# Dense units shifted in both attention blocks, tile 1 of a gated projection four units behind, rows summed later

## The reference

```python
def first_block(...):
    mod = silu(c) @ w_ada + b_ada                      # six rows of 1024: shifts, scales, gates
    h = modulate(rms_norm(x, g_mix), sh_m, sc_m)
    qa, ka, va, qb, kb, vb, gate_logits = split(h @ w_in)
    oa = moba_attention(qa, ka, va, rel_bias)          # 8 heads, softmax with a bias
    ob = stick_breaking_attention(qb, kb, vb)          # 8 heads, cumulated log sigmoids
    mixed = (g_a * (oa @ w_br_moba) + g_b * (ob @ w_br_sb)) @ w_out
    x = x + gt_m * mixed
    ... gated convolution feed-forward, final norm
def second_block(...):                                 # layer 0 even, layer 1 odd
    for l in range(2):
        x = x + 0.5 * rmsnorm(swiglu(...))
        m = even_mixer(...) or odd_mixer(...)          # even: differential attention, then attention
        x = x + rmsnorm(m)                             # over the top 64 keys of an indexer
        x = x + 0.5 * rmsnorm(swiglu(...))
```

## Time and profile before

| | before |
|---|---|
| median of 3 runs | 1549.98 us (1548.85 to 1555.81) |
| the profiled execution | 1548.18 us, span of its instructions 1546.4 us |
| TensorE matmul busy | 1462.1 us, 95% |
| VectorE, ScalarE, GpSimd busy | 926.5, 735.7, 57.7 us |
| mean granted clock of TensorE | 0.976 |
| DMA | 274.29 MB, 177 GB/s |

### The profile page before, as it was taken

The page is one execution under the profiler, slowest core; times in us unless marked ns, Lnnn a source line. Parts: engine busy times, 40 slices in busy tenths (PEclk is TensorE's granted clock), DMA queues, the critical chain, the costliest instruction groups (busy, mean ns, idle before and its releaser), DMA issues.

```text
span 1546.4 us, 17969 instructions
## 1 busy us (share of the span) xinstructions
PE 1462.1 (95%) x6791; PEld 1198.4 (77%) x6791; DVE 926.5 (60%) x1128; ACT 735.7 (48%) x990; POOL 57.7 (4%) x104
## 2 busy tenths in 40 slices
PE   5998988899998999999789999999999999999998
PEld 5877867688876888877567888878888778788886
DVE  5675667678866644458955654556454455565443
ACT  1555544555553544355444644445444465554441
POOL 2000000000000000013100000000000100000000
PEclk9998989899999999999879999999999999999999
DMA  8964545277652755535214655546555373356550
GB/s 319 322 223 152 197 176 182 80 244 243 218 190 96 245 190 183 175 99 168 102 55 150 219 189 191 190 150 218 190 191 190 123 211 110 136 168 227 181 174 28
DMA packets 180311, 274.29 MB, mean 177 GB/s; under 512 B 6242, under 2 KB 120674, under 8 KB 180226
## 3 DMA queue, kind: packets, MB, share of 16 engines
q1 hardware_dynamic: 176976, 263.45, 50.9%
q0 software_dynamic: 1824, 6.57, 1.4%
q10 hardware_dynamic: 1425, 3.12, 0.6%
HBM read 272.05 MB, written 1.06 MB: 177 GB/s over the span
## 4 chain that ended last, share of the span: by engine, by line
PE 80%; DVE 10%; issue 4%; ACT 4%; DMA 1%; POOL 0%; DVEq 0%; POOLq 0%; SPq 0%; ACTq 0%
PE psum L2030 24%; PE psum L2032 24%; PE psum L2031 24%; DVE w_lo L1652 2%; PE psum L2225 2%; ACT w_hi L1465 1%; DMA raw<-in_w_ada_dram 1%; PE psum L2101 1%; DVE ada_acc L1693 1%; PE psum L2154 1%; PE psum L2153 1%; PE psum L2169 1%; DVE scr L1992 1%; PE psum L2195 1%; PE psum L2196 0%
## 5 line engine op out<-in xcount | busy, mean ns | idle before, releaser
L1652 DVE TENSOR_TENSOR w_lo<-raw,w_hi 128x2048 fp32r<-128x2048 f32 x157 | 358.3, 2285 | 197.1 <-ACT w_hi L1465 196.7
L2030 PE MATMUL psum<-w_hi,hT_hi 128*128 128x512 f32 x1000 | 400.5, 400 | 10.9 <-DVE w_lo L1652 3.5
L2032 PE MATMUL psum<-w_hi,hT_lo 128*128 128x512 f32 x1000 | 392.4, 392 | 0.0
L2031 PE MATMUL psum<-w_lo,hT_hi 128*128 128x512 f32 x1000 | 391.8, 392 | 0.0
L1465 ACT ACTIVATE w_hi<-raw 128x2048 fp32r<-128x2048 f32 x157 | 299.5, 1909 | 161.6 <-PE psum L2032 95.2
L2030 PEld LDWEIGHTS psum<-w_hi,hT_hi 128*128 128x128 f32 x1000 | 189.8, 190 | 57.9 <-issue 16.9
L2032 PEld LDWEIGHTS psum<-w_hi,hT_lo 128*128 128x128 f32 x1000 | 189.5, 189 | 40.7
L2031 PEld LDWEIGHTS psum<-w_lo,hT_hi 128*128 128x128 f32 x1000 | 189.8, 190 | 36.7
L2030 PE MATMUL psum<-w_hi,hc_hi 128*128 128x512 f32 x256 | 101.8, 398 | 4.8 <-DVE hc_lo L1657 4.0
L1652 DVE TENSOR_TENSOR lo_at<-raw,hi_at 128x2048 fp32r<-128x2048 f32 x35 | 80.2, 2291 | 39.1 <-ACT hi_at L1465 39.1
L1652 DVE TENSOR_TENSOR lo_qk<-raw,hi_qk 128x2048 fp32r<-128x2048 f32 (+1 forms) x35 | 79.2, 2264 | 38.6 <-ACT hi_qk L1465 38.6
(11 more groups left out here) (197 smaller groups left out, 2006.6 us busy)
## 6 DMA issues: line engine op xcount, KB each, us to landing
raw<-in_ffn_wg_dram SPq DMA_DIRECT2D x88, 512.0 KB, 3.7
raw<-in_ffn_wu_dram SPq DMA_DIRECT2D x88, 512.0 KB, 4.7
raw<-in_ffn_wd_dram SPq DMA_DIRECT2D x44, 1024.0 KB, 4.9
raw<-in_w_ada_dram SPq DMA_DIRECT2D x24, 1024.0 KB, 5.5
raw<-in_w_up_dram SPq DMA_DIRECT2D x44, 512.0 KB, 5.1
raw<-in_w_in_dram SPq DMA_DIRECT2D x20, 1024.0 KB, 5.1
raw<-in_even_w_in_dram SPq DMA_DIRECT2D x12, 1024.0 KB, 5.0
raw<-in_odd_w_in_dram SPq DMA_DIRECT2D x12, 1024.0 KB, 5.1
```

The source lines that it names most:

```text
L1652: nc.vector.tensor_tensor(lo_of(s), raw_of(s), hi_of(s).bitcast(F32), ALU.subtract).then_inc(lo_ready, 1)
L2030: nc.tensor.matmul(o, a_hi, b_hi, start=start, stop=False)
L2031: nc.tensor.matmul(o, a_hi, b_lo, start=False, stop=False)
L2032: return nc.tensor.matmul(o, a_lo, b_hi, start=False, stop=stop)
```

## The change

- `WIDE` starts at unit 24, so `w_out`'s units can use the two extra slots and be split ahead.
- `sb_heads`: the second filler of a step runs only from the second pair on, and the lists are reordered (13 lists for 14): unit, two row parts, unit; the last gate unit moves between `sb_keep` and `sb_cum` of the last pair. The transposes of the first attention's output move between the two units of the last gate and from banks 6, 7 to 2, 3.
- `ada_next` sums the previous row after the second part of a row instead of after the first.
- `w_out`: all four units are multiplied for tile 0 first; tile 1 of all four stands in the pieces of `cross`, which now prepares the high half of one unit less before tile 0's chain (`early=1`).
- `out_rest`: the transposes stand between tile 0 and tile 1 of one unit.
- Even block: TensorE waits for the indexer's turn at the first `idx` step, not behind the turn; the two units of the second attention's values (`first_of(5)`, `second_of`) and the turn of its keys move into the last steps of the differential attention.

```diff
-WIDE = ((28, 98), (112, 182), (194, 227))
+WIDE = ((24, 98), (112, 182), (194, 227))
@@ sb_heads
-            filler()
             if i:
+                filler()
                 for m in before:
                     pl.add("sb_pv", m=m, v=v_col + m * HD, uses=o, v_ready=v_ready)
@@ cross
-    def cross(chain, head, pieces):
+    def cross(chain, head, pieces, early=2):
-            pl.hi_to(head.u0 + 2)
+            pl.hi_to(head.u0 + early)
         b(0)
         pieces[1]()
+        if head:
+            pl.hi_to(head.u0 + 2)
@@ ada_next
-            adasum(sum_due.pop(), bank)
+            adasum(sum_due.pop(0), bank)
         ada(n, part)
-        sum_next(bank)
         if part:
+            sum_next(bank)
             sum_due.append(n)
@@
-        fb += [[first], [second], [ada_next] if i else [ada_next, ada_next]]
+        fb += [[first], [ada_next] if i else [ada_next, ada_next], [second]]
-        turn("scr", ("uses", moba_out), None, None, 0, 4, (6, 7), GM)
+        turn("scr", ("uses", moba_out), None, None, 0, 4, (2, 3), GM)
-    fb += [[turn_moba], [second_branch]]
+    fb[10].append(turn_moba)
+    fb += [[second_branch]]
@@ w_out
-            if (n, half) != (1, 1):
+            if (n, half) == (0, 0):
                 pl.split_ahead(u)
-            if n == 0:
-                product_step("proj", part)
-                sum_next(half)
-            else:
-                product_step("proj", part, ts=(0,), inc=y[half][0])
-                last_two.append(part)
+            product_step("proj", part, ts=(0,), inc=y[half][0] if n else None)
+            behind.append(part)
+            if (n, half) == (0, 1):
+                sum_next(0)
+                sum_next(0)
@@ pieces
-        lambda: None,
-        lambda: product_step("proj", last_two[0], ts=(1,)),
-        lambda: product_step("proj", last_two[1], ts=(1,), ks=(0, 1), inc=None),
-        lambda: product_step("proj", last_two[1], ts=(1,), ks=(2, 3))])
+        lambda: product_step("proj", behind[0], ts=(1,)),
+        lambda: product_step("proj", behind[1], ts=(1,)),
+        lambda: product_step("proj", behind[2], ts=(1,)),
+        lambda: product_step("proj", behind[3], ts=(1,))], 1)
@@ out_rest
-            product_step("proj", p)
+            product_step("proj", p, ts=(0,), inc=None)
             turn(src, ("scr_ready", n_scr[0]), None, None, 4, 4, (4, 5), GO)
+            product_step("proj", p, ts=(1,))
@@ even block
-                     [topk(6)], [topk(7), fill_turn(4, "bk", 12)]]
+                     [topk(6), first_of(5)], [topk(7)], [second_of], [fill_turn(4, "bk", 12)]]
-            fills = [[first_of(5)], [second_of, lambda: pl.add("diffnorm", ...)], [], [], [],
+            fills = [[], [lambda: pl.add("diffnorm", ...)], [], [], [],
@@ idxturn, idx on TensorE
-                    for use in a["uses"]:
-                        wait_read(pe, use)
+                    if h == 0:
+                        for u in a["ready"]:
+                            wait_read(pe, u)
```

More of the change, by code:

```diff
@@ L874, in build_plan @@
     v = scr_version()
-    last_two = []
+    behind = []
     for n in range(2):
@@ L1034, in build_plan @@
             r0 = rope(pl, 0, 8, HD, u0)
-            pl.add("idxturn", uses=[pl.use(2), pl.use(3)], after=("rope_ready", r6))
+            idx_turned = [pl.use(2), pl.use(3)]
+            pl.add("idxturn", uses=idx_turned, after=("rope_ready", r6))
             u2, parts = ep(2)
@@ L1039, in build_plan @@
             for h in range(4):
-                pl.add("idx", h=h, use=pl.use(h % 2))
+                pl.add("idx", h=h, use=pl.use(h % 2), ready=idx_turned)
             turns_of("aq", 0, 0, 2, ("rope_ready", r0))
@@ L1078, in build_plan @@
             sd["n"] = pl.var()
-            fills = [[first_of(5)], [second_of, lambda: pl.add("diffnorm", uses=o_diff, st=sd, v=v, n=sd["n"])], [], [], [],
+            fills = [[], [lambda: pl.add("diffnorm", uses=o_diff, st=sd, v=v, n=sd["n"])], [], [], [],
                      [turn_first("scr", ("scr_ready", v))], [out_first(W["even_w_out"][0])]]
```

## The result

The kernel after takes 1556.91 us (median of 20 runs, 1550.32 to 1562.81), the kernel before beside it 1553.38 (20 runs, 1548.85 to 1556.02): ratio 1.0023, 95% interval 1.0013 to 1.0033. It is 3.5 us slower where 1.3 us less was forecast. The profiled execution took 1559.1 us, its span 1557.4, at a mean granted clock of 0.974.

The account below looks back on a forecast made before the run. The prediction took TensorE (95% busy) to carry the time, with its losses set by VectorE's in-order queue. Terms +4.5 +4.3 -1.4 -7.2 -1.5 = -1.3 on one execution of 1548.2 gave 1547 us, range 1535 to 1557.

Parts of the forecast that it names:

- Step 5: Even block's attentions, value-projection units moved earlier: second attention starts later but ends sooner, -7.2 us, bounds -11 and -2.
- steps 4 and 6: Indexer turn's wait moved behind a dense unit, -1.4 us; both output projections' waits covered by twelve matmuls, -1.5 us.
- step 3: Gated projection, weight slots earlier and tile 1 behind: low halves delay the mixing, new waits outweigh the gap removed, +4.3 us.
- step 2: First block's second attention: a 3.4 us gap, small gaps, then a 4.6 us bank 3 wait; +4.5 us including step 1.
- Step 1: First block's first attention, rows summed later: TensorE waits for bank 3 behind VectorE's product and add, +0.7 us.
- The faster one: Rival: mixing in the gated projection not late behind the low halves, step 3 is -7.1, total 1535.5 us; chance 0.25.
- The slower one: Rival: new gaps (3.1 us one, tile 1's three, second even attention's start) cost 3.0 us of clock each; 1555.9 us; chance 0.2.
- The rule weighed in the prediction: Idle gaps lower the clock, so don't empty the second even attention's start; step 5 then -2, sum 1552.1 us.

Follow-up runs that it names:

- sums_part: Kernel before with only the modulation rows summed one row later (the `ada_next` hunk), fillers as before: ratio 0.9993 to the kernel before.
- attention_parts: Kernel before with only the first block's reordered second-attention fillers, its turn's banks and the rows summed later: ratio 1.0029, 4.5 us slower.
- Log_behind_unit: attention_parts with the logarithm step, from the second pair of heads on, issued behind the dense unit: ratio 1.0002 to the kernel before.
- gated_part: Kernel before with only tile 1 of the gated output projection behind tile 0 and five weight slots four units earlier: ratio 1.0033, 5.1 us slower.
- even_part: Kernel before with only the even block's two value-projection units moved into the first attention's last steps: ratio 0.9982, in a second measurement 0.9978.
- even_norm_later: even_part with the normalisation of the first attention's output issued one head later: ratio 0.9952 to the kernel before, 7.5 us less.
- Even_out_earlier: even_part with the first attention's output turn and the dense output-projection unit behind it one head earlier: ratio 0.9971 to the kernel before.

## Why the prediction was wrong, by its steps

**What the whole miss consists of.** +3.5 us measured for -1.3 forecast. Step 5 gave 3.8 to 4.4 us less than forecast and is the step that failed; steps 4 and 6 together gave 1.0 less, step 3 cost 0.8 more, step 2 came out at its sum by luck. Measured alone they miss by 6 us, the whole by 4.8; the difference is within the intervals.

**Step 1, right in its gap.** The gap is 4.05 us for 3.33, so +0.7. TensorE goes on at 133.62, but this execution is 0.55 us later than the first one of the kernel before already at the transposes at 100.01 (100.56), and absolute times of two executions cannot be compared that closely. In sums_part the gap of 2.10 us goes as well, and the part alone is not slower.

**Step 2, right in sum by luck, wrong in the middle.** Forecast: +4.5, end 229.9 (its own terms, 212.3 + 14.4 + 3.0, add to 229.7). The trace ends at 229.27, 3.9 later than before or 3.3 without the 0.55, and attention_parts measured +4.5. The gap of 3.4 came as 3.32. But the small gaps of 1.0, 1.3 and 1.4 were 6.01 (4.77 in two other traces), 1.76 and 2.21, and the 4.6 us at bank 3 did not come. The step followed VectorE's queue and not ScalarE's: the next gate's unit needs banks 6 and 7 read, which with one unit between two gates becomes a wait. The prediction says that all the gaps of the kernel before end on VectorE; three of them are marked "issue" in the earlier trace rows, and that they do was its inference. Two errors of 6.3 and 4.6 us, of opposite sign, left the sum standing. Log_behind_unit shows both.

**Step 3, right.** Forecast gaps 3.1, 1.9, none, then 1.9, 2.3, 1.7; found 3.03, 1.54, none, 1.74, 1.90, 1.57. The 1.0 us for the clock behind the first of them was not seen in the kernel after (1.06 us for eight transposes), but was in gated_part (1.94). The 12 matmuls behind 292.90 ran at 1.2 GHz, 2.5 us that the step did not charge; in gated_part they did not. +4.3 forecast, 5.1 measured by the ratio and 4.3 by the stage of gated_part's trace.

**Step 4 right, step 6 a third.** -2.9 forecast together, -1.9 measured. Step 4's 1.5 us came. Of step 6's 1.5 only 0.5 did: the next gap was forecast to take part of it back, and took more, growing from 1.89 to 2.82 us.

**Step 5, the term that failed.** Forecast -7.2, measured -2.8 and -3.4. The start was right: TensorE begins the second attention at 784.16 in even_part, 1.04 of which it had before that block (708.95 for 707.91), so 783.1 against 782.7 forecast. The gap of 3.6 was 2.41 there (4.31 in the kernel after). What was wrong is the stretch behind the start: 30.3 us forecast, 33.9 found, with a gap that is 1.2 us shorter, so 4.8 us are to be explained. "Its small products run at 1.2 GHz until about 799" is the sentence that failed, about 800 on the clock of even_part. In even_part TensorE ran at half speed from 788.21 until 807.9, into its only dense unit at 804.77: the unit took 7.1 us and not 5.6 (1.5 us), and the 4.7 us of small products between 800 and the unit took twice their time (an estimate from these rows, 2.4 us). 0.9 us is not assigned. In the kernel before the products were slow only from 800.54 to 807.2, since two units ran ahead of them. So the price of slow clock over a stretch without dense units was put too low. The gap is a separate term: even_norm_later takes it away (2.4 us of idle time) and leaves the clock at 0.73, and so reaches the 7 us forecast by a way that the forecast did not have. Even_out_earlier leaves the gap and saves 1.5 us of slow work in its trace; its ratio is not apart from even_part's.

**The level.** Of the 10 us between 1546.9 and 1556.9, 4.8 are the change (+3.5 for -1.3) and 5.2 the level: the sum was made against one execution of 1548.2, while the kernel before has its median at 1553.4. The three runs shown reached from 1548.85 to 1555.81, so this was to be seen.

**The rivals.** The faster one (the cover holds in the gated projection) is refuted: gap 3.03. The slower one, 1555.9, is nearest in time, but it was made against the low level; its +7.7 us are twice the +3.5 measured. Its mechanism came in two of its three places: in the second even attention, and behind 292.90 (2.5 us). It did not come behind 248.44 (the eight transposes in 1.06 us).

The rule weighed in the prediction, that idle gaps bring the clock down (the Trainium skill, TensorE: Matmul & The Clock Gate, Why this matters for your kernels), gave 1552.1 as its sum by the weaker bound of -2 for step 5, a change of +3.9. That is close to the measured +3.5. In the kernel after the rows agree with the rule: the scores at 801.08 take 0.49 us, those at 807.40, behind the gap of 4.31 us, 0.76. In even_part they do not need that gap: the clock was down from 788.21, behind gaps under 0.8 us, and in even_norm_later, with no longer gap left, it stayed at 0.73. I had the row for a clock that falls and chose the larger gain.

## What to carry to other kernels

When a unit is moved up to another that uses the same banks, read the queue of the engine that empties them, not only the queue that the old gap named: here ScalarE stood idle 9 us with the reading of two finished banks behind a step that could not start. When cover is taken away from a stretch, ask what long step of another engine stood under it (6.2 us of normalisation) and move that too; that one edit added 4.0 to 4.7 us to the 2.8 to 3.4 of the two dense units. What it is worth in the kernel before, where the gap is 1.17 us, was not tried. Where a stretch loses its dense units, charge 1.2 GHz up to and into the next unit (in even_part from 788.2 to 807.9), not up to the old place. And sum against the median of many runs, not against one execution.

## What the runs showed of the chip

The clock falls or not behind gaps of one size. The gap of 3.03 us in front of the mixed transposes is the same in the kernel after and in gated_part; TensorE's timeline of gated_part shows these eight at 1.2 GHz, 1.94 us against 1.06, and what decides it is open:

```profile
244.76 1.94 PE L2102 MATMUL psum<-cst,scr 128*128 128x128 f32 x8 [3.03 <-DVE scr L1934]
```

And it can fall behind gaps under 0.8 us (even_part, 788.21). With waits that differ by less than 1 us in sum, two executions of the kernel before were 6 us apart. Of ScalarE's table loads, the Trainium skill (ScalarE: Activation LUTs, What ACT_TABLE_LOAD costs) gives 1.28 us and a drain of 1.38 beside. The rows above show the 1.28, and 0.01 to 0.02 us between a load and the work on either side of it. No drain is seen there, so a load costs about half of what that page would put on it; between 158 and 168 there are three, in the next pair of heads two.
